# A hybrid decoder step: another order of the DeltaNet rounds, and gated expert outputs joined with split statistics

## The reference

```python
def _gated_delta_chunked(q, k, v, g, beta, s0):      # per head, c rows at a time
    def step(s, xs):
        ...
        a = strictly_lower(kb @ k.T * decay)
        sol = triangular_solve(eye + a, [v * beta, kb * exp(G)])
        u = sol_v - sol_k @ s
        o = (q * exp(G)) @ s + (q @ k.T * decay) @ u
        s = s * exp(g_last) + (k * exp(g_last - G)).T @ u
def _deltanet_mixer(...):
    qkv = silu(causal_conv(h @ w_in));  o = _rms_norm(o, norm_g) * silu(z);  return o @ w_out
def _moe(h, ...):
    gates = two experts' softmax shares, normalised, per token
    act = silu(gu[..., :256]) * gu[..., 256:] * gates
    y = einsum('tef,efd->td', act, w_down)
x = _layer_norm(ALPHA * x + (1 + gate_f) * y, ln_g, ln_b)
```

## Time and profile before

| what | us |
|---|---|
| median of 3 runs (2099.69, 2101.22, 2122.41) | 2101.22 |
| the profiled execution: its time, its span | 2105.92, 2104.1 |
| PE busy, DVE busy, ACT busy, POOL busy in the span | 1820.2, 794.4, 379.0, 357.6 |
| comb0 (first gather to the first instruction of delta) | 921.4 to 965.6 |
| delta (first matmul to the last turn) | 965.7 to 1743 |
| comb1 (first gather to the last vector instruction) | 2056.9 to 2100.6 |

### The profile page before, as it was taken

How to read it: one execution, slowest core, us unless ns; L and a number is a source line. 1 busy time by engine, 2 the same in 40 slices (tenths; PEclk the granted TensorE clock), 3 DMA queues, 4 the chain that set the end, 5 groups by cost and what they waited for, 6 DMA issues and landing times. The chain is left out here.

```text
span 2104.1 us, 37009 instructions
## 1 busy us (share of the span) xinstructions
PE 1820.2 (87%) x15669; PEld 970.9 (46%) x15669; DVE 794.4 (38%) x1655; ACT 379.0 (18%) x839; POOL 357.6 (17%) x461
## 2 busy tenths in 40 slices
PE   6999999999999678957979989988989888949990
PEld 4344444444434333324556665765665463433320
DVE  0233332323424320034665455546544442450006
ACT  1001000000000011124332242232223110002112
POOL 0020110201103100022421022031113000320006
PEclk9999999999999879987999999999999999969995
DMA  9546657465551299988431034033124548158993
GB/s 327 190 164 232 257 200 256 143 230 200 171 201 50 86 390 401 399 302 266 135 97 48 12 114 126 9 112 92 43 59 170 195 158 270 60 215 320 401 359 137
DMA packets 237630, 399.62 MB, mean 190 GB/s; under 512 B 17993, under 2 KB 94017, under 8 KB 237410
## 3 DMA queue, kind: packets, MB, share of 16 engines
q1 hardware_dynamic: 231514, 375.75, 51.3%
q0 software_dynamic: 5952, 21.50, 2.7%
HBM read 303.71 MB, written 93.51 MB: 189 GB/s over the span
## 5 line engine op out<-in xcount | busy, mean ns | idle before, releaser
L686 PE MATMUL bank<-ring,hT 128*128 128x512 f32 x704 | 319.5, 601 | 1.9 <-DVE ret_qk L904 1.9
L1361 PE MATMUL bank<-hT,ring 128*128 128x272 f32 x768 | 217.0, 417 | 0.0
L686 PEld LDWEIGHTS bank<-ring,hT 128*128 128x128 f32 x704 | 129.6, 191 | 170.0 <-issue 169.8
L2541 PE MATMUL bank<-expert_w,exp_xT 128*32 128x512 f32 x1152 | 178.1, 626 | 15.3 <-DMA expert_w<-in_moe_w_gu_dram 11.4
L1361 PEld LDWEIGHTS bank<-hT,ring 128*128 128x128 f32 x768 | 140.7, 197 | 33.6 <-issue 8.9
L1355 PE MATMUL bank<-ring,hT 128*128 128x512 f32 x256 | 124.8, 616 | 0.0
L3354 PE MATMUL bank<-ring,oT 128*128 128x512 f32 x248 | 114.3, 622 | 0.8 <-PEq L580 0.8
L2541 PEld LDWEIGHTS bank<-expert_w,exp_xT 128*32 128x32 f32 x1152 | 47.9, 115 | 126.4 <-issue 121.2
L2637 DVE TENSOR_TENSOR exp_a<-bank,exp_sg 128x256 f32<-128x256 f32 x24 | 10.2, 424 | 218.9 <-ACT exp_sg L2619 218.9
L978 DVE SCALAR_TENSOR_TENSOR ret_Ss<-ret_Ss,ret_sdec,bank 128x512 f32<-128x512 f32 x64 | 45.0, 744 | 121.3 <-PE bank L772 121.3
L2054 DVE SCALAR_TENSOR_TENSOR dn_y<-dn_pre,dn_conv,dn_y 128x568 f32<-128x568 f32 x96 | 89.1, 928 | 3.4
(11 more groups left out here) (531 smaller groups left out, 2719.3 us busy)
## 6 DMA issues: line engine op xcount, KB each, us to landing
expert_w<-in_moe_w_gu_dram SPq DMA_DIRECT2D x24, 2048.0 KB, 16.9
ring<-in_w_ada_dram SPq DMA_DIRECT2D x20, 2048.0 KB, 9.5
expert_outputs<-ret_zeros SPq DMA_DIRECT2D x15, 2048.0 KB, 10.4
expert_w<-in_moe_w_down_dram SPq DMA_DIRECT2D x24, 1024.0 KB, 17.4
ret_Ss<-in_state_ret_dram SPq DMA_DIRECT2D x32, 512.0 KB, 5.2
out_dram<-ret_Ss SPq DMA_DIRECT2D x32, 512.0 KB, 3.3
oT<-in_moe_w_gu_dram SPq DMA_DIRECT2D x8, 2048.0 KB, 20.6
ring<-in_dn_w_in_dram SPq DMA_DIRECT2D x8, 2048.0 KB, 9.2
```

Of the source, the lines that this page charges most:

```text
L686: last = pe.matmul(ps[u % 2][:, :], core.hT[:, k, tok(t)], core.ring[:, core.slot[w], k, :], start=(k == 0), stop=(k == KD - 1))
L1361: mm = pe.matmul(ps[U % 2][:, 0:HALF], core.ring[:, core.slot[w], k, c * P:(c + 1) * P], core.hT[:, k, half * HALF:(half + 1) * HALF], sta ...
L2541: last = pe.matmul(ps[v][G * j:G * (j + 1), :], xT[:, v, k, G * j:G * (j + 1)], wgu[of[j] % SLOTS][:, k, :], start=(k == 0), stop=(k == KD ...
```

## The change

Three parts.

1. **The order in delta.** C5 is split: OG is its part on DVE, C5 what PE and ACT do. S3 is split into UE (DVE spreads), S3 (PE) and SU (DVE adds to the states). The solve has places of its own (`SOLVE`) where it was spread evenly. Two units of the next group's projections (16 steps) are kept for the end of each group: 12 steps before its last C5 and 4 behind it. In the last group six OP steps stand in front of the last C5. The convolution is cut into two halves, two steps of `mm` apart.
2. **Weights inside the experts.** The shares of the two experts are spread to slots by one more sum of matmuls in the routing (`slot_weight`), and L2637 becomes one instruction that multiplies by the share too. Joining is then a plain addition.
3. **Statistics over three engines.** The sum of x comes with the DVE instruction that makes x; DVE divides it (128x1); ACT takes the squares of the deviations with their sum, and adds the epsilon; POOL does only the power. comb1 multiplies (x - mean) by ln_g while ACT and POOL work, and one DVE instruction scales and adds ln_b; POOL writes no more 128x1024 tile. In comb0 the prompt rows and the gate are loaded in the last passes of the experts (`first_rows_in`, into hT and oT).

The diff, cut to its core:

```diff
@@ -1090,11 +1090,12 @@
-                out += [("CV", x + i), ("C1", x + i), ("C4", x + i - 1), ("C2", x + i), ("C5", x + i - 1), ("C3", x + i)]
-            return out + [("C4", x + NC - 1), ("C5", x + NC - 1)]
+                out += [("CV", x + i), ("C1", x + i), ("C4", x + i - 1), ("C2", x + i), ("OG", x + i - 1), ("C3", x + i),
+                        ("C5", x + i - 1)]
+            return out + [("C4", x + NC - 1), ("OG", x + NC - 1), ("C5", x + NC - 1)]
...
-            return [("S1", g, hp), ("S2", g, hp), ("S3", g, (hp, 0)), ("S3", g, (hp, 1))]
+            return [("S1", g, hp), ("S2", g, hp)] + [(what, g, (hp, half)) for half in range(2) for what in ("UE", "S3", "SU")]
...
@@ -1121,10 +1122,12 @@
-                         at={2: (0.05, 0.12, 0.2), 3: (0.55, 0.65, 0.72, 0.8, 0.86, 0.92, 0.98)})
+                         at={0: SOLVE, 2: (0.04, 0.09, 0.13, 0.18, 0.181, 0.23, 0.28),
+                             3: (0.55, 0.62, 0.67, 0.71, 0.76, 0.761, 0.81, 0.86, 0.89, 0.94, 0.99)})
             c = c_steps(g)
-            return out + merge(b_steps(2 * g + 1), c[:10]) + c[10:]
-
+            return out + merge(b_steps(2 * g + 1), c[:11], at={0: SOLVE}) + c[11:]
+
+        SOLVE = (0.02, 0.11, 0.18, 0.25, 0.31, 0.38, 0.44, 0.51, 0.57, 0.69, 0.79, 0.87, 0.95)
...
-                    head = 2 * KD if g == 1 else 0
-                    yield from mm[:head]
-                    mm = mm[head:]
-                    yield from merge(group(g - 1), mm, at={1: [SPREAD * (i + 0.5) / len(mm) for i in range(len(mm))]})
-                else:
-                    even = lambda a, b, n: [a + (b - a) * (i + 0.5) / n for i in range(n)]
-                    yield from merge(group(g - 1), mm, LAST, OUT, at={1: even(0, 0.29, len(mm)), 2: even(0.3, 0.96, len(LAST)),
-                                                                      3: even(0.29, 0.5, 2 * KD) + even(0.5, 0.99, 2 * KD)})
...
+            yield from products(first[1], first[1] + ahead)
+            for g in range(1, G):
+                mm, *body = list(products(first[g] + ahead, first[g + 1])), *group(g - 1)
+                yield from merge(body[:-1], mm, at={1: [SPREAD * (i + 0.5) / len(mm) for i in range(len(mm))]})
+                fill = list(products(first[g + 1], first[g + 1] + ahead))
+                yield from fill[:-4]
+                yield body[-1]
+                yield from fill[-4:]
+            even = lambda a, b, n: [a + (b - a) * (i + 0.5) / n for i in range(n)]
+            mm, body = list(products(first[G] + ahead, first[G + 1])), group(G - 1)
+            end = 1 - 1 / len(body)
+            yield from merge(body, mm, LAST, OUT, at={1: even(0, 0.2, len(mm)), 2: even(0.25, 0.94, len(LAST)),
+                                                      3: even(0.21, 0.5, 2 * KD) + even(0.5, 0.96, KD + 2) + [end] * (KD - 2)})
...
+                        rest(item[1] - 1)
                 else:
...
+                    if taps[0] == 0:
+                        dve.wait_ge(s["pre_parts"], parts(F + 1))
+                        if F:
+                            dve.wait_ge(s["act_done"], 2 * F)
+                        chain(dve.tensor_scalar(y[:, 0:n], pre[:, F % 2, 0:n], t.conv[:, ch, 0:1], None, ALU.mult))
+                    for k in taps:
+                        if k == 0:
+                            continue
                         ins = dve.scalar_tensor_tensor(y[:, 0:n], pre[:, F % 2, k:k + n], t.conv[:, ch, k:k + 1], y[:, 0:n],
                                                        ALU.mult, ALU.add)
                         if k < 3:
                             chain(ins)
-                    ins.then_inc(s["conv_done"], 1)
+                        else:
+                            ins.then_inc(s["conv_done"], 1)
...
-                    if what == "C5":
+                    if what == "OG":
...
-                    if what == "S3":
+                    if what == "UE":
...
+                    if what == "SU":
+                        hp, half = l
+                        n = 2 * g + hp
...
+def first_rows_in(sp, core, x_from, sem):
+
+    sp.wait_ge(core.ada_out, core.OUT["routing"])
+    sp.dma_start(first_gate(core), core.dram["mod"][0:1, 5 * D:6 * D].broadcast_to([P, D])).then_inc(sem, 16)
+    for t in range(NPT):
+        sp.dma_start(core.hT[:, :, tok(t)], x_from(t).rearrange("p (k c) -> p k c", k=KD)).then_inc(sem, 16)
...
+        pe.wait_ge(shares_done, 1)
+        for i in range(2 * NT):
+            n = rows(i % NT)
+            last = pe.matmul(ps[7][:, MAXT:2 * MAXT], at_lane[0:n, i, :], own[0:n, i, :], start=(i == 0), stop=(i == 2 * NT - 1))
+        last.then_inc(shares_ps, 1)
...
+        chain(dve.tensor_tensor(own[:], bc(tile[:], MAXT), row(tiles, 2 * NT), ALU.is_equal))
+        dve.tensor_tensor(own[:], own[:], bc(plan.weight[:].rearrange("p j t -> p (j t)"), MAXT), ALU.mult).then_inc(shares_done, 1)
+        dve.wait_ge(shares_ps, 1)
+        chain(dve.tensor_copy(plan.slot_weight[:], ps[7][:, MAXT:2 * MAXT]))
...
-                    dve.tensor_tensor(a[:, v, :], ps[v][:, DE:2 * DE], sg[:, v, :], ALU.mult).then_inc(s["a_done"], 1)
+                    share = plan.slot_weight[:, i:i + 1] if isinstance(i, int) else plan.slot_weight[:, bass.ds(i, 1)]
+                    dve.scalar_tensor_tensor(a[:, v, :], ps[v][:, DE:2 * DE], share, sg[:, v, :], ALU.mult, ALU.mult
+                                             ).then_inc(s["a_done"], 1)
...
-                def join(n):
-                    t, v = ORDER[n], n % 2
-                    A, B, X, gate, g, b = part(n)
-                    dve.wait_ge(s["weighed"], n + 1)
-                    chain(dve.scalar_tensor_tensor(A, B, weight(n, 1), A, ALU.mult, ALU.add))
+                def join(t):
+                    A, B, X, gate, g, b = part(t)
+                    dve.wait_ge(s[f"got{t}"], 32)
+                    chain(dve.tensor_tensor(A, A, B, ALU.add))
                     chain(dve.scalar_tensor_tensor(B, gate, 1.0, A, ALU.add, ALU.mult))
-                    chain(dve.scalar_tensor_tensor(X, X, ALPHA, B, ALU.mult, ALU.add))
-                    for c in range(2):
-                        chain(dve.bn_stats(stats[:, v, c, :], X[:, c * W:(c + 1) * W]))
-                    dve.bn_aggr(mom[:, t, :], stats[:, v].rearrange("p c s -> p (c s)")).then_inc(s["moments"], 1)
-                    dve.wait_ge(s["moments"], n + 1)
+                    chain(dve.scalar_tensor_tensor(X, X, ALPHA, B, ALU.mult, ALU.add, accum_out=sums[:, t:t + 1]))
+                    dve.tensor_scalar(mean[:, t:t + 1], sums[:, t:t + 1], -1.0 / D, None, ALU.mult).then_inc(s["mean_done"], 1)
+                    dve.wait_ge(s["mean_done"], READY.index(t) + 1)
+                    dve.scalar_tensor_tensor(A, X, mean[:, t:t + 1], g, ALU.add, ALU.mult).then_inc(s["centred"], 1)
...
+                    chain(dve.bn_aggr(mom[:], ps[7][:, P:P + 24]))
+                    dve.sem_inc(s["mean_done"], 1)
+                    dve.scalar_tensor_tensor(A, X, mom[:, 0:1], g, ALU.subtract, ALU.mult).then_inc(s["centred"], 1)
+
+                def finish(t):
+                    A, B, X, gate, g, b = part(t)
+                    dve.wait_ge(s["rstd_done"], READY.index(t) + 1)
+                    dve.wait_ge(s["centred"], READY.index(t) + 1)
+                    dve.scalar_tensor_tensor(X, A, rstd[:, t:t + 1], b, ALU.mult, ALU.add).then_inc(s["x_done"], 1)
...
+                finish(0)
+                join(NPT)
+                finish(1)
...
+                finish(NPT)
+                finish(2)
+                finish(3)
...
+                def deviate(n):
+                    t = READY[n]
+                    A, B, X, gate, g, b = part(t)
+                    act.wait_ge(s["mean_done"], n + 1)
+                    if t < NPT:
+                        chain(act.activation(B, X, ACT.Square, bias=mean[:, t:t + 1], accum_out=squares[:, t:t + 1]))
+                        act.activation(var[:, t:t + 1], squares[:, t:t + 1], ACT.Identity, bias=core.eps[:, 0:1], scale=1.0 / D
+                                       ).then_inc(s["var_done"], 1)
+                    else:
+                        act.activation(var[:, t:t + 1], mom[:, 1:2], ACT.Identity, bias=core.eps[:, 0:1]).then_inc(s["var_done"], 1)
...
-                    dve.wait_ge(s["weighed"], t + 1)
-                    chain(dve.scalar_tensor_tensor(A, B, plan.weight[0:n, 1, t:t + 1], A, ALU.mult, ALU.add))
-                    if t == 0:
-                        dve.wait_ge(s["gate_in"], 32)
-                    chain(dve.scalar_tensor_tensor(B, gate[0:n, m, :], 1.0, A, ALU.add, ALU.mult))
-                    dve.wait_ge(x_in[t], 16)
-                    chain(dve.scalar_tensor_tensor(X, X, ALPHA, B, ALU.mult, ALU.add))
-                    for c in range(2):
-                        chain(dve.bn_stats(stats[0:n, v, c, :], X[:, c * W:(c + 1) * W]))
```

(13 more changed lines are left out.)

210 lines of the change are left out of this document (81 added, 129 removed).

## The result

| what | before | after |
|---|---|---|
| median of 4 runs, us | 2104.03 | 2037.74 |
| ratio, 95% interval | | 0.9654 (0.9622 to 0.9686) |
| profiled execution, its span | 2105.92, 2104.1 | 2031.6, 2029.8 |

The forecast of 2040 was 2 us off, and its range held the time. The profiled execution of after was the quickest of its four, so its span fell by 74.3 us where the medians fell by 66. The sum of the forecast came out for another reason than its terms: delta gave more than was counted, comb0 gave nothing, and the stretches with routing and experts took back 4 us that the forecast had put at nothing. The table reads each stage from the first and last start of the instructions that bound it, so that it adds up to the span.

The account below looks back on a forecast made before the run. PE was taken to bound delta, less 84 us idle, and DVE comb0. Delta's idle time -38, clock -12, comb1 -8 and comb0 -5 made -63: 2043 from the profiled execution, 2038 from the median, stated as 2040, range 2018 to 2078.

Parts of the forecast that it names:

- C5 and the filled ends: Delta: PE work moved ahead of the turns covers the 34.7 us of waits for `dn_ob`; -31 us, bounds -17 to -35.
- S3: Delta: the spread ahead of a halved convolution cuts PE's 19.4 us of waits for `dn_ue`; -12, 7 left, bounds -4 to -19.
- Solve: Delta: the halved convolution block saves 3 us; uneven `SOLVE` places add one 1 us wait in eight solves, +8 (0 to +16).
- The clock: Delta: with most long waits gone, PE work at the lower clock is won back; -12 us, bounds 0 to -20.
- three stretches like that of 1174 to 1182: Delta: eight busy microseconds at granted clock 0.51 did the work of four; three such stretches taken back make the -12.
- comb1: Last join: DVE's path from 2063.24 would end near 2092.4 against 2100.56; -8 us, bounds 0 to -9.
- comb0: First join: shorter join -6.5, less competition up to -1.5, early loads mostly hidden 0 to +3.5; -5, bounds -9 and +3.
- Costed at nothing: Experts, routing, delta's last group: the share in L2637, `slot_weight` products and SP's added `op_in` wait, all hidden, 0 us.
- A: Delta: waits move to the solve and DVE's queue, half of 46 us returns, clock gives nothing; 2065 to 2070; chance 0.20.
- B: Group ends: convolutions and POOL's `km` ahead of OG lengthen the chain, only the joins' -13 remains; 2088 to 2093; chance 0.08.
- C: Delta: OG and UE block DVE's queue in 32 places, 1.1 us each, making it slower; 2109 to 2146; chance 0.05.
- D: Joins: DVE instructions with a sum take 1.2 us more each; +5 to +11, near 2050; chance 0.07.

Follow-up runs that it names:

- the second of these kernels: The kernel before, with 4 to 28 idle unit-matrix products in each of 16 delta waits, cut so that no block outlasts its wait: ratio 0.9901, delta 761.9 us.

## Why the prediction came out right, point by point

- **C5 and the filled ends** (-31): 34.7 to 1.6, -33. The cover was sized by records: 5.8 forecast, 5.67 measured. Undoing the fill left 18.9 us of waits and 19 us more of delta. The turns moved behind C3 were given about 7 of the 31 (20.2 is for the group ends, 3.9 for the last turn); undoing them returned 4 us of waits.
- **S3** (-12, left 7): 19.4 to 3.9, -15.5. I counted only the four waits over 2.5 us; the short ones went too. By the undone kernel the split and its places are worth 31 us with the clock, against 19 for the fill and 6 for the turns. I had C5 for the main part; it is no larger than S3. That the parts add up isn't shown.
- **Solve** (-3 and +8): the named waits (`dn_TT` 5.5, `dn_X` 3.4, DVE's queue 3.2, together 12.1) became 18.1 (`dn_TT` 13.2, `dn_X` 0.5, `dn_TTs` 4.4): +6 against +5. That new solve waits come was right; that `SOLVE` makes them was wrong, for without it they are as long and delta is 9 us longer, 6.5 of it before a load of the sample states.
- **The clock** (-12, bounds 0 to -20): **the term mis-sized**. Measured -26.5 in PE's busy time over delta, beyond its bound, and 20 to 26 in the kernel whose waits were only filled. The step that failed was to take back three stretches like that of 1174 to 1182 where the waits were some 20. The cap over all of delta was there to be read (47 us from the mean of 0.94), and half of it came back. The Trainium skill, "TensorE: Matmul & The Clock Gate", Part 1, puts the ramp penalty at under 1% of a typical span. It says so of the slow matmuls at a kernel's start, so the forecast's cap of 21 us was not the page's to give; the clock that fell again behind some 20 waits cost 20 to 26 us here, 1.0 to 1.2% of the span.
- The waits named above, -42.6 (forecast -38), and busy time, -26.5 (forecast -12), make 69 of delta's 72.3 us; the rest is idle time outside these rows.
- **comb1** (-8): -7.7, by the forecast's sum. Neither the square with its sum (1.15 + 0.19) nor POOL's power held DVE for more than 0.44 us.
- **comb0** (-5, bounds -9 and +3): **the step that was wrong**. From the last copy to delta it came to +2.1 in the profile of the changed kernel, and 46.9 to 51.4 in seven profiles with these loads, mean 48.9, against 49.3 to 50.5, mean 49.7, in four with the old joins: -0.8. The step that failed is that the early loads would mostly be hidden. The gather slipped by 2.2 to 5.9 us in these seven, because the last stores landed late behind them. The forecast's bytes, 6.5 us at 386 GB/s, would account for all of that; the loads in pieces also held SyncE for 10.6 to 13.6 us, and the gather slipped most in the two kernels that held it longest (13.6). Bytes or pieces: no run loads whole rows in the experts, so it stays open. From the first gather to delta comb0 gained 3.8 us, where 8 were counted (6.5 for the join, 1.5 for the rows out of the gathers' way); why the join gives less isn't shown. "No DVE read in 8 x 128 in the trace": it costs nothing, 1.23 us.
- **Costed at nothing**: the second sum in the routing takes 5.15 us on PE beside the first rows' gather; from the first sum to the first turned rows it is 14.3 us before and 14.2 after in layer 1. The share in L2682 makes it 0.48 instead of 0.42, and DVE still waits 206.8 us before it. So neither is seen to cost anything where it stands; yet the stretches with routing and experts are longer by 3.3 and 2.3 us on average, a term that the forecast put at nothing and whose cause stays open.
- **Rivals**: A asked for half of the 46 us to return, over 30 us of solve waits, and for nothing from the clock; the solve waits are 18.1, 6 more than before, and the clock gave 26.5. B needed DVE's convolutions ahead of OG; the chain of the group's end kept its length. C needed 2.5 us in each of 32 places; OG waits at most the same 1.12 as before (9.9 us in 9 places, 8.8 in 8 before) and UE not at all. D: 1.22 to 1.23 with the sum, as without. The Trainium skill, "Vector Engine (DVE) Microarchitecture Reference", section 7, would have it at half the throughput for two non-bf16 sources; this fp32 instruction with both in SBUF and a sum takes 1.23 us, the same as without a sum, and the measurement decides. The forecast was wrong that one source takes 1.22 as well: a TENSOR_SCALAR of 128x1024 with one source takes 0.81 us in both traces (L3249, L3272). So two sources are slower than one here, and the sum adds 0.08.

So 2040 came about by errors that cancelled, which is luck: 22 us too little in delta; 7 too much in comb0 and 4 in the stretches before and between. On the profiled execution that leaves the forecast 11 us short (-63 for -74.3); the medians gained 66, and hid it.

## What to carry to other kernels

Price a removed wait with the half clock behind it: here 46 us of idle time came with 20 to 26 us of slow work, and filling waits with idle products measures that share before anything is moved. When an engine walks one list with its partners, split a step at its hand-over (spread, multiply, add) before moving work in bulk; of the parts undone singly, the split of these small steps was worth the most. When you move a DMA, look at what is queued behind it, its issues and its landing: a store issued on time landed 5.7 us later than before. And an idle row without a releaser may be a load: compare its end with the landings.

## What the runs showed of the hardware

- Products that do nothing, put where TensorE idled, raised the granted clock of delta from 0.94 to 0.98 and 0.99; the second of these kernels was 1.0% (0.7 to 1.3%) faster without any of its work moved.
- The four loads of 512 KB took 10.6 to 13.6 us to issue in pieces of 512 bytes at the end of the experts, in seven kernels, and 13.8 in comb0. The first of the four took 0.6 to 0.8, a later one up to 8.5. Three such loads and one of 128 KB in rows of 4 KB took 1.8 to 1.9.
- With the DMA engines' share at 1.05 up to 924, a store of 512 KB landed 8.4 us after its issue; with a share of 0.51 it took 2.7.
- DVE's scaling of 4 x 128x128 took 3.13 to 3.14 us beside two POOL instructions of 128x512 in all five cases of both traces: the first two of its instructions took 1.33 to 1.35 each instead of 0.34. In 26 of the other 27 cases, with POOL idle, the four took 1.13 to 1.14; in one, beside 0.39 us of POOL, 1.32.
